# Output-weight parts drawn into step 7, late conditioning pieces moved behind the first output tiles

## Chip, cores and metric

One core of a Trainium2 chip. The metric is the device time of the slowest core in microseconds, here of the only one. The engines are TensorE (PE, its weight loads PEld), VectorE (DVE), ScalarE (ACT), GpSimd (POOL) and SyncE (SP, which issues most DMAs).

## What is computed

One layer of a conditioned decoder trunk in float32, for a prompt of 1024 rows and 8 samples of 8 rows (1088 columns), 1024 channels:

```python
mod = silu(c) @ w_ada + b_ada                      # 6 x 1024 rows: shift, scale, gate for mixer and MLP
h = rms_norm(x, g_mix) * (1 + sc_m) + sh_m
u_val, u_glu, u_rec, u_y = split(h @ w_in + b_in)  # 4 x 512 columns
ya = silu(layer_norm(causal_dwconv31(u_val * sigmoid(u_glu))))
cb = causal_dwconv4(u_rec)
a = exp(-8 * sigmoid(cb @ w_ga) * softplus(-lam))  # gates are block-diagonal
h_t = a * h_(t-1) + sqrt(1 - a^2) * sigmoid(cb @ w_gx) * cb
x = x + gt_m * (concat[ya, h * gelu(u_y)] @ w_out)
h2 = rms_norm(x, g_ffn) * (1 + sc_f) + sh_f
x = x + gt_f * (relu(h2 @ w_up)^2 @ w_down)
y = rms_norm(x, g_final)                           # the last conv rows and h are returned as states too
```

## The kernel before

Every large product is made of three: each float32 operand is split into a high part (ACT, a copy to fp32r, `hi`, line 603) and a low part (POOL, raw minus high, `lo`, line 404), and TensorE adds high x high, high x low and low x high. The order on every engine is written out by hand in five programs (`sync`, `gpsimd`, `scalar`, `vector`, `tensor`) that meet at semaphores.

**In-projection.** Eight steps m = 0..7 of two strips (s = 0, 1) of 128 output columns, each over three chunks c of 384, 384 and 320 token columns. Steps 0 to 3 give value and GLU gate of a quarter j of group A, steps 4 and 5 the recurrent branch, 6 and 7 the GELU branch. Between strips stand pieces of the conditioning product (`ada_piece`, w_ada split too), the means for the LayerNorm (`mean_a`, step 6) and the variances (`var_a`, step 7, line 1530). ACT reads each chunk from PSUM (lines 707 to 710). POOL multiplies value and gate (`product`, line 428), DVE makes the 31 taps of convolution A, one tile j after another (lines 1167 to 1178), then the four taps of convolution B.

**Between step 7 and the output product.** ACT makes the standard deviation (`deviation`, line 811), DVE its reciprocal and the normalised conv_a (`normalise`, lines 1217 and 1218). TensorE makes the gates of the recurrence (`recurrent_gates`), ACT their tanh, a = exp and tanh (`recurrence`, lines 816 to 828), POOL the square a2 (line 498; one buffer, so square j waits for q_done j), DVE the gated input and q (`gated_input`, lines 1224 and 1228), ACT the roots (line 856), DVE the recursion in two halves (`recur`, lines 1262 to 1278), and the low parts of the activations (lines 1283 and 1292). TensorE turns five groups of state rows (`turn_state`, bank 6), read out by DVE (`staged`). Meanwhile the eight blocks k of w_out are loaded into two slots of raw, and split (`w_out_hi`, `w_out_lo`): block k's load waits for the low part of block k - 2.

**Late pieces.** The last 16 of 48 rows of the conditioning are not split: eight `late_piece` q, each eight float32 products of a 128x128 weight block with nine columns (line 1622), that is 16 instructions, into bank 7. DVE adds the bias (line 1312) and makes the second scales sc_f; POOL spreads the MLP gate to the samples.

**Output product and second norm.** `gates` spreads gt_m over the tokens, then nine tiles t of 128 tokens, `tile_product` over eight blocks k (lines 1677 to 1684). Tiles 0 to 3 need half 0 of the activations. Behind tile 1 the last states h_end are turned (line 1710). DVE adds each tile to x (`add_tile`), ACT and DVE make the norm, TensorE turns its rows from behind tile 2 on (`turn`, line 1434), `modulate` applies sc_f. Eight MLP blocks follow.

The program below prints the functions with the lines of the profile.

## Time and profile before

| | |
|---|---|
| median of 3 runs | 1257.45 us (1257.35 to 1257.83) |
| profiled execution | 1255.39 us, span 1253.6 us |
| TensorE busy (matmul) | 1191.2 us, 95% |
| TensorE weight loads | 1070.9 us, 85% |
| DVE busy | 725.8 us, 58% |
| ACT busy | 385.3 us, 31% |
| POOL busy | 346.1 us, 28% |
| mean granted TensorE clock | 0.974 |

The span runs from the first to the last instruction; 1.8 us of the profiled execution lie around it. Busy shares are averages over stages with different limits: what an edit is worth is read from the waits and the timelines of its own stage.
### The profile page before, as it was taken

What the parts mean: (1) busy time and instruction counts of PE and PEld (TensorE: products, weight loads), DVE (VectorE), ACT (ScalarE), POOL (GpSimd) and SP (SyncE); (2) the same over time, 40 slices, a digit from 0 to 9 for tenths busy, and PEclk for the clock granted to TensorE, in tenths of its full rate; (3) what the DMA queues carried; (4) which work ended last, traced back from release to release, by engine and by line L of the source; (5) the groups of instructions that cost most, each with busy time, mean ns of one, the idle gap of its engine ahead of it and who ended that gap; (6) DMA issues with size and microseconds to landing.
All of it is one profiled execution on the core that took longest, in us unless ns stands there. A gap on an engine that the chain in (4) does not pass through costs nothing.

```text
span 1253.6 us, 16249 instructions
## 1 busy us (share of the span) xinstructions
PE 1191.2 (95%) x6255; PEld 1070.9 (85%) x6255; DVE 725.8 (58%) x841; ACT 385.3 (31%) x681; POOL 346.1 (28%) x209
## 2 busy tenths in 40 slices
PE   6789999999869998999999999999999999999996
PEld 2589999988658888989989989989989988988985
DVE  2749999994896555435445445445345345345457
ACT  4842433423762434402302302301301301301322
POOL 0236888440641103302301301301301301301300
PEclk9798999999879998999999999999999999999998
DMA  9524334403415101201201201201201201201112
GB/s 300 176 67 118 101 111 125 118 17 95 127 51 177 35 1 54 69 13 35 85 18 33 84 17 33 84 17 33 84 17 33 84 17 33 84 17 33 50 45 98
DMA packets 80811, 87.36 MB, mean 70 GB/s; under 512 B 3816, under 2 KB 61440, under 8 KB 80771
## 3 DMA queue, kind: packets, MB, share of 16 engines
q1 hardware_dynamic: 78661, 84.77, 21.7%
q10 hardware_dynamic: 2110, 2.05, 0.6%
q8 instruction: 26, 0.43, 0.1%
q14 instruction: 14, 0.11, 0.0%
HBM read 81.72 MB, written 5.08 MB: 69 GB/s over the span
## 4 chain that ended last, share of the span: by engine, by line
PE 86%; DVE 7%; ACT 2%; DMA 2%; issue 2%; POOL 1%; SPq 1%; ACTq 0%; DVEq 0%; POOLq 0%
PE ps L1522 15%; PE ps L1524 15%; PE ps L1523 15%; PE ps L1677 11%; PE ps L1680 11%; PE ps L1678 11%; DMA ada<-in_w_ada 2%; PE ps L1684 1%; PE ps L1683 1%; PE ps L1414 1%; PE ps L1415 1%; PE ps L1530 1%; DVE rstd L1217 1%; DVE tmp_a L1273 1%; DVE gel L1278 0%
## 5 line engine op out<-in xcount | busy, mean ns | idle before, releaser
L1522 PE MATMUL ps<-act_hi,w_hi 128*128 128x384 f32 (+1 forms) x1152 | 380.2, 330 | 10.0 <-POOL w_lo L404 5.6
L1524 PE MATMUL ps<-act_hi,w_lo 128*128 128x384 f32 (+1 forms) x1152 | 377.5, 328 | 0.0
L1523 PE MATMUL ps<-act_lo,w_hi 128*128 128x384 f32 (+1 forms) x1152 | 377.4, 328 | 0.0
L1522 PEld LDWEIGHTS ps<-act_hi,w_hi 128*128 128x128 f32 x1152 | 217.9, 189 | 12.8 <-issue 6.4
L1523 PEld LDWEIGHTS ps<-act_lo,w_hi 128*128 128x128 f32 x1152 | 217.9, 189 | 1.8
L404 POOL TENSOR_TENSOR wb_lo<-raw,wb_hi 128x1024 fp32r<-128x1024 f32 x40 | 98.6, 2474 | 433.3 <-ACT wb_hi L603 433.1
L1524 PEld LDWEIGHTS ps<-act_hi,w_lo 128*128 128x128 f32 x1152 | 217.7, 189 | 0.0
L404 POOL TENSOR_TENSOR w_lo<-raw,w_hi 128x1024 fp32r<-128x1024 f32 x48 | 118.2, 2466 | 334.9 <-ACT w_hi L603 277.8
L1322 DVE TENSOR_TENSOR ps<-ps,gt_p 128x1024 f32<-128x1024 f32 x72 | 88.7, 1232 | 206.8 <-PE ps L1680 206.7
L1677 PE MATMUL ps<-wb_hi 128*128 128x512 f32 x512 | 199.4, 389 | 1.1 <-ACT gt_s L904 1.1
L1678 PE MATMUL ps<-wb_lo,wb_hi 128*128 128x512 f32 x512 | 199.2, 389 | 0.0
L1352 DVE TENSOR_TENSOR relu<-relu 128x384 f32<-128x384 f32 (+1 forms) x96 | 74.7, 778 | 198.7 <-ACT relu L948 198.7
L1680 PE MATMUL ps<-wb_hi,wb_lo 128*128 128x512 f32 x512 | 157.7, 389 | 0.0
L603 ACT ACTIVATE wb_hi<-raw 128x1024 fp32r<-128x1024 f32 x40 | 41.1, 1051 | 360.9 <-PE ps L1684 319.2
L1175 DVE SCALAR_TENSOR_TENSOR ps<-ga,caw,ps 128x1024 f32<-128x1024 f32 x112 | 134.2, 1280 | 0.0
L1677 PEld LDWEIGHTS ps<-wb_hi 128*128 128x128 f32 x512 | 96.1, 188 | 21.1 <-ACT gt_s L904 1.3
L1680 PEld LDWEIGHTS ps<-wb_hi,wb_lo 128*128 128x128 f32 x512 | 96.1, 188 | 20.0
L1678 PEld LDWEIGHTS ps<-wb_lo,wb_hi 128*128 128x128 f32 x512 | 96.1, 188 | 19.7
L948 ACT ACTIVATE relu<-ps 128x384 f32<-128x384 f32 (+1 forms) x96 | 45.2, 471 | 186.6 <-PE ps L1524 177.5
L1324 DVE TENSOR_TENSOR x<-x,ps 128x1024 f32<-128x1024 f32 x72 | 88.0, 1222 | 2.5
L1677 PE MATMUL ps<-wb_hi,act_hi 128*128 128x512 f32 x128 | 51.2, 400 | 11.9 <-DVE act_lo L1292 11.9
L413 POOL TENSOR_TENSOR aw_lo<-raw_ada,aw_hi 128x1024 fp32r<-128x1024 f32 x24 | 57.8, 2427 | 0.0
(229 smaller groups left out, 1287.1 us busy)
## 6 DMA issues: line engine op xcount, KB each, us to landing
raw<-in_w_up SPq DMA_DIRECT2D x32, 512.0 KB, 4.0
raw<-in_w_down SPq DMA_DIRECT2D x32, 512.0 KB, 3.3
raw_ada<-in_w_ada SPq DMA_DIRECT2D x24, 512.0 KB, 3.9
ada<-in_w_ada SPq DMA_DIRECT2D x8, 1024.0 KB, 14.9
x<-in_x_prompt SPq DMA_DIRECT2D x16, 512.0 KB, 8.2
raw<-in_w_in SPq DMA_DIRECT2D x16, 512.0 KB, 5.3
ada_late<-in_w_ada SPq DMA_DIRECT2D x8, 512.0 KB, 4.7
out<-x SPq DMA_DIRECT2D x8, 512.0 KB, 2.6
```

The costliest lines, as they stand in the source:

```text
L404: pool.tensor_tensor(dst, raw[:, slot, :], hi.bitcast(F32), ALU.subtract).then_inc(lo_ready, 1)
L413: pool.tensor_tensor(aw_lo[:, slot, :], raw_ada[:, slot, :], aw_hi[:, slot, :].bitcast(F32), ALU.subtract).then_inc(ada_lo, 1)
L1175: dve.scalar_tensor_tensor(out=out if k == KA - 1 else a, in0=win, scalar=w, in1=a, op0=ALU.mult, op1=ALU.add).then_inc(conva_tap, 1)
L1322: dve.tensor_tensor(src, src, gt_p[:, :], ALU.mult).then_inc(gated, 1)
L1324: dve.tensor_tensor(x2[:, t, :], x2[:, t, :], src, ALU.add).then_inc(rmw_done, 1)
L1352: dve.tensor_tensor(f, r, r, ALU.mult).then_inc(r2_done, 1)
L1522: mm(out, wh, xh, start=(k == 0), stop=False)
L1523: mm(out, wh, xl, start=False, stop=False)
L1524: last = mm(out, wl, xh, start=False, stop=(k == KD - 1))
L1677: mm(out, ah, wh, start=(k == 0), stop=False)
L1678: mm(out, ah, wl, start=False, stop=False)
L1680: last = mm(out, al, wh, start=False, stop=end)
```

## The change

product(0) goes from POOL to DVE, in front of convolution A. In step 7 the variances stand one strip earlier each (behind s = 0 c = 1, s = 0 c = 2 and s = 1 c = 0), and ACT makes the deviations and the first two high parts of w_out behind the first chunk of the last strip. DVE normalises all three chunks in one go. POOL splits w_out blocks 0 and 1 first, waits for all three normalisations (a2 now lies in rstd), and keeps two blocks ahead of the squares; the sample gates follow the squares. ACT takes blocks 2 to 5 between the recurrences, 4 and 5 behind q 1 and q 2. All loads of w_out are on SP. TensorE makes each recurrent gate ahead of the late piece that stood before it. Of the eight late pieces 0 to 2 stay, 3 to 5 stand behind output tile 0, 6 and 7 behind tile 1 ahead of the h_end transposes; the second scales (`late_scales`) stand behind DVE's addition of tile 1, as do the waits for them.

```diff
--- before.py
+++ after.py
@@ -232,7 +232,7 @@
         g_t = [tmp_b[:, j, :] for j in range(J)]
-        a2 = sg
+        a2 = rstd
         gx_t = [tmp_a[:, j, :] for j in range(J)]
@@ -323,16 +323,23 @@
             load_out(0)
+            load_out(1)
             sp.wait_ge(strip_a, 2 * J * NC)
...
             load_late(0, 2)
-            load_out(1)
+            load_out(2)
+            load_out(3)
             sp.wait_ge(strip_b, 2 * J * NC)
...
             load_late(0, 3)
-            for n in range(4):
-                load_out(n + 2)
-                load_late(1, LATE_ORDER[n])
+            load_out(4)
+            load_late(1, 0)
+            load_out(5)
+            load_out(6)
+            load_late(1, 2)
+            load_out(7)
+            load_late(1, 1)
+            load_late(1, 3)
             for a in range(2, LATE):
@@ -457,7 +464,6 @@
-            product(0)
             step(0)
@@ -491,21 +497,25 @@
             pool.wait_ge(var_done, NC)
+            w_out_lo(0)
+            w_out_lo(1)
+            pool.wait_ge(xs_done, NC)
             for j in range(J):
-                w_out_lo(j)
+                if j == 1:
+                    pool.wait_ge(st_tr, 1)
+                w_out_lo(j + 2)
                 pool.wait_ge(a_done, j + 1)
...
                 pool.tensor_tensor(a2[:, :], a_t[j], a_t[j], ALU.mult).then_inc(a2_done, 1)
-                if j == 2:
-                    pool.wait_ge(st_tr, 3)
-                    pool.wait_ge(ada_tr, ADA0 + ADA_S)
-                    pool.wait_ge(ada_evac, ADA0 + ADA_S)
-                    sample_gate(0, M_GTM)
+            pool.wait_ge(st_tr, 3)
+            pool.wait_ge(ada_tr, ADA0 + ADA_S)
+            pool.wait_ge(ada_evac, ADA0 + ADA_S)
+            sample_gate(0, M_GTM)
             pool.wait_ge(evac_a, 2 * J * NC)
...
             pool.wait_ge(q_done, J)
-            for k in range(J, KD):
-                w_out_lo(k)
+            w_out_lo(6)
+            w_out_lo(7)
             for j in range(J):
@@ -734,7 +744,7 @@
                 for c in range(NC):
-                    if c == 2 and 2 <= m <= ADA_S + 1:
+                    if c == (1 if m == 2 * J - 1 else 2) and 2 <= m <= ADA_S + 1:
                         group_out(turned, 7, 0)
@@ -783,6 +793,16 @@
+            def deviation(c):
+
+                t0, w = c * CH, CW[c]
+                act.wait_ge(var_done, c + 1)
+                act.activation(rstd[:, t0:t0 + w], ps[:, 5 + c, 0:w], ACT.Sqrt, bias=eps[:, :]).then_inc(sd_done, 1)
+
+            def w_out_hi(k):
+
+                hi(W_OUT0 + k, k % 2, wb_hi[:, k, :], 16 * ((W_OUT0 + k) // 2 + 1))
+
@@ -793,7 +813,15 @@
-                step(q + J + J // 2, out_a, lambda c, bank: gelu_out(c, bank, 2 * q + 1, evac_b))
+
+                def out_b(c, bank):
+                    gelu_out(c, bank, 2 * q + 1, evac_b)
+                    if last and c == 0:
+                        for n in range(NC):
+                            deviation(n)
+                        w_out_hi(0)
+                        w_out_hi(1)
+                step(q + J + J // 2, out_a, out_b)
@@ -804,12 +832,6 @@
-            def deviation(c):
-
-                t0, w = c * CH, CW[c]
-                act.wait_ge(var_done, c + 1)
-                act.activation(rstd[:, t0:t0 + w], ps[:, 5 + c, 0:w], ACT.Sqrt, bias=eps[:, :]).then_inc(sd_done, 1)
-
@@ -828,24 +850,16 @@
-            def w_out_hi(k):
-
-                hi(W_OUT0 + k, k % 2, wb_hi[:, k, :], 16 * ((W_OUT0 + k) // 2 + 1))
-
-            for c in range(NC):
-                deviation(c)
-            w_out_hi(0)
-            w_out_hi(1)
+            w_out_hi(2)
             recurrence(0)
+            w_out_hi(3)
             recurrence(1)
-            w_out_hi(2)
+            act.wait_ge(q_done, 1)
+            w_out_hi(4)
             recurrence(2)
-            w_out_hi(3)
+            act.wait_ge(q_done, 2)
+            w_out_hi(5)
             recurrence(3)
-            def load_out(k):
-
-                act.wait_ge(lo_ready, W_OUT0 + k - 1)
-                act.dma_start(raw[:, k % 2, :], w_out[0, k * P:(k + 1) * P, :]).then_inc(raw_in[k % 2], 16)
@@ -881,18 +895,12 @@
             roots(0)
-            w_out_hi(4)
-            w_out_hi(5)
+            w_out_hi(6)
+            w_out_hi(7)
             roots(1)
-            load_out(6)
             ya(0)
-            load_out(7)
-            yb_hi(0, 0)
-            yb_hi(0, 1)
-            w_out_hi(6)
-            yb_hi(0, 2)
-            w_out_hi(7)
-            yb_hi(0, 3)
+            for j in range(J):
+                yb_hi(0, j)
             ya(1)
@@ -912,13 +920,14 @@
             act.dma_start(h_sample[0], h_st[1:9, :]).then_inc(staged_out, 16)
-            act.wait_ge(sc_done, 2)
             for t in range(NT):
...
                     strip_hi(W_MLP0 + 1, 1, strip_b, 0)
+                if t == 1:
+                    act.wait_ge(sc_done, 2)
                 if t > 0:
@@ -1179,6 +1188,11 @@
             dve.wait_ge(sa_cp, 2)
+            dve.wait_ge(evac_a, NC)
+            dve.wait_ge(evac_b, NC)
+            dve.tensor_tensor(ga[:, 0, KA - 1:GA_P], ga[:, 0, KA - 1:GA_P], sg[:, 0:SEQ], ALU.mult).then_inc(ga_ready, 1)
+            dve.tensor_tensor(ga_s[:, 0, :, KA - 1:GA_S], ga_s[:, 0, :, KA - 1:GA_S],
+                              sg[:, SEQ:TOK].rearrange("p (b t) -> p b t", t=TB), ALU.mult).then_inc(ga_ready, 1)
             with dve.Fori(0, J) as j:
@@ -1234,12 +1248,11 @@
-            normalise(0)
+            for c in range(NC):
+                normalise(c)
             staged(0, stage[0:KA - 1, 2, :], KA - 1)
-            normalise(1)
             gated_input(0)
             staged(1, stage[0:half_rows, 0, :], half_rows)
-            normalise(2)
             gated_input(1)
@@ -1307,13 +1320,15 @@
-            dve.wait_ge(late_used, 4 * LATE)
-            b_late = par[:, C_BADA + ROW_L:C_BADA + 48].unsqueeze(2).broadcast_to([P, 48 - ROW_L, 9])
-            dve.tensor_tensor(mod[:, ROW_L:48, :], ps[:, 7, 0:9 * (48 - ROW_L)].rearrange("p (r c) -> p r c", c=9),
-                              b_late, ALU.add).then_inc(late_mod, 1)
-            dve.wait_ge(ada_evac, ADA0 + ADA_S)
-            dve.wait_ge(late_mod, 1)
-            scales(sc_f, M_SCF, C_GFFN)
+            def late_scales():
+
+                dve.wait_ge(late_used, 4 * LATE)
+                b_late = par[:, C_BADA + ROW_L:C_BADA + 48].unsqueeze(2).broadcast_to([P, 48 - ROW_L, 9])
+                dve.tensor_tensor(mod[:, ROW_L:48, :], ps[:, 7, 0:9 * (48 - ROW_L)].rearrange("p (r c) -> p r c", c=9),
+                                  b_late, ALU.add).then_inc(late_mod, 1)
+                dve.wait_ge(ada_evac, ADA0 + ADA_S)
+                dve.wait_ge(late_mod, 1)
+                scales(sc_f, M_SCF, C_GFFN)
@@ -1332,12 +1347,14 @@
             dve.wait_ge(gt_cp, 2)
-            dve.wait_ge(sc_done, 2)
             for t in range(NT):
...
                 add_tile(t, out_bank(t), t)
+                if t == 1:
+                    late_scales()
+                    dve.wait_ge(sc_done, 2)
                 if t > 0:
@@ -1559,8 +1576,8 @@
                             mean_a(c)
-                        if last and s == 1:
-                            var_a(c)
+                        if last and 1 <= 3 * s + c <= NC:
+                            var_a(3 * s + c - 1)
@@ -1629,19 +1646,17 @@
             turn_state(0, 6, KA - 1, lambda j: tail_p[:, j, :])
+            recurrent_gates(1)
             late_piece(0)
             turn_state(1, 6, 4 * (KA - 1), lambda j: tail_a[:, j, 0:120])
-            recurrent_gates(1)
+            recurrent_gates(2)
             late_piece(1)
             turn_state(2, 6, 4 * (KA - 1), lambda j: tail_a[:, j, 120:240])
-            recurrent_gates(2)
-            late_piece(2)
+            recurrent_gates(3)
             pe.wait_ge(tails, 2)
             turn_state(3, 6, KB - 1, lambda j: tail_bp[:, j, :])
-            recurrent_gates(3)
+            late_piece(2)
             turn_state(4, 6, NB * (KB - 1), lambda j: tail_b[:, j, :])
-            for q in range(3, 4 * LATE):
-                late_piece(q)
@@ -1704,6 +1719,8 @@
                              (lambda: turn(2, 2, xn[:, 0, :])) if t == 4 else None)
+                for q in ((3, 4, 5), (6, 7))[t] if t < 2 else ():
+                    late_piece(q)
                 if t == 1:
```

## Rows read from the trace of the kernel before

**Rows 1.** TensorE's waits, whole span: line <- releaser: us in total, times, longest

```profile
PE ps L1677 <- DVE act_lo L1292: 11.9, 1, 11.9
...
PE ps L1522 <- POOL w_lo L404: 5.6, 1, 5.6
```

**Rows 2.** timeline of POOL after step 0 (start us, us, engine, operation)

```profile
90.36 2.00 POOL L428 TENSOR_TENSOR ga<-ga,sg 128x1024 f32<-128x1024 f32 x1 [17.07 <-ACT sg L710]
...
92.59 4.70 POOL L404 TENSOR_TENSOR w_lo<-raw,w_hi 128x1024 fp32r<-128x1024 f32 x2
```

**Rows 3.** timeline of ACT after step 0

```profile
89.97 0.31 ACT L710 ACTIVATE sg<-ps,par 128x64 f32<-128x64 f32 x1
90.17 2.00 ACT L778 ACTIVATE w_hi<-raw 128x1024 fp32r<-128x1024 f32 x2
```

**Rows 4.** timeline of DVE: first tap and last addition of convolution A

```profile
92.92 1.35 DVE L1167 TENSOR_SCALAR ps<-ga,caw,par 128x1024 f32 x1 [15.43 <-POOL ga L430]
...
255.92 1.22 DVE L1178 TENSOR_TENSOR conv_a<-conv_a,ps 128x1024 f32 x1
```

**Rows 5.** timeline of TensorE's weight loads: first mean product

```profile
257.31 0.68 PEld L1530 LDWEIGHTS ps<-conv_a,mean_w 128*128 128x128 f32 x3
```

**Rows 6.** chain that ended last, inside step 7 (start us, us, what)

```profile
298.20 2.58 PE ps L1530 x8
```

**Rows 7.** timeline of ACT from the end of step 7 on

```profile
306.33 1.47 ACT L811 ACTIVATE rstd<-ps,eps 128x384 f32<-128x384 f32 x3
...
311.00 0.90 ACT L816 ACTIVATE tmp_a<-ps,hb 128x768 f32<-128x768 f32 x1
...
316.07 0.90 ACT L816 ACTIVATE tmp_a<-ps,hb 128x768 f32<-128x768 f32 x1
```

**Rows 8.** timeline of POOL in the same stretch

```profile
308.91 2.37 POOL L404 TENSOR_TENSOR wb_lo<-raw,wb_hi 128x1024 fp32r<-128x1024 f32 x1 [29.48 <-ACT wb_hi L603]
...
330.43 2.00 POOL L498 TENSOR_TENSOR sg<-tmp_b 128x1088 f32<-128x1088 f32 x1 [3.89 <-DVE tmp_a L1228]
...
344.40 5.97 POOL L404 TENSOR_TENSOR wb_lo<-raw,wb_hi 128x1024 fp32r<-128x1024 f32 x2 [4.13 <-ACT wb_hi L603]
```

**Rows 9.** timeline of DVE in the same stretch

```profile
306.94 2.55 DVE L1217 RECIPROCAL rstd<-rstd 128x384 f32<-128x384 f32 x1 [15.92 <-ACT rstd L811]
309.53 3.37 DVE L1218 TENSOR_TENSOR conv_a<-conv_a,rstd 128x1536 f32<-128x1536 f32 x1
...
320.80 1.28 DVE L1228 SCALAR_TENSOR_TENSOR tmp_a<-sg,tmp_a 128x1088 f32<-128x1088 f32 x1
...
331.47 2.11 DVE L1224 SCALAR_TENSOR_TENSOR tmp_b<-tmp_a,ga 128x1088 f32<-128x1088 f32 x1 [0.58 <-ACT tmp_a L819]
...
341.34 1.28 DVE L1228 SCALAR_TENSOR_TENSOR tmp_a<-sg,tmp_a 128x1088 f32<-128x1088 f32 x1
...
343.49 0.69 DVE L1266 SCALAR_TENSOR_TENSOR tmp_b<-tmp_a,tmp_b 128x512 f32<-128x512 f32 x1
...
364.64 2.48 DVE L1292 TENSOR_TENSOR act_lo<-gel,act_hi 128x512 fp32r<-128x512 f32 x4
```

**Rows 10.** timeline of TensorE: late pieces, then tiles 0 to 2

```profile
336.04 13.98 PE L1622 MATMUL ps<-c_t,ada_late 128*128 128x9 f32 x80
...
367.23 0.77 PE L1677 MATMUL ps<-wb_hi,act_hi 128*128 128x512 f32 x1 [11.91 <-DVE act_lo L1292]
...
390.85 0.48 PE L1677 MATMUL ps<-wb_hi,act_hi 128*128 128x512 f32 x1
...
401.84 1.03 PE L1434 MATMUL ps<-ident,xn 128*128 128x128 f32 x8
```

**Rows 11.** busy us (x instructions) of PE, PEld, DVE, ACT, POOL; clock; DMA

```profile
99.00:100.00 1.00, 1.00 (x5) 1.00 (x4) 1.00 (x2) 0.00 (x0) 1.00 (x2) 0.50 0.93 266
336.00:339.00 3.00, 3.00 (x30) 3.00 (x28) 0.76 (x1) 2.98 (x4) 3.00 (x2) 1.00 0.00 0
341.00:349.00 8.00, 8.00 (x39) 8.00 (x39) 7.75 (x10) 5.96 (x9) 4.53 (x2) 0.50 0.56 155
```

## The prediction

> **What bounds the kernel now.** I read the share of each engine first, then TensorE's waits, then the timelines around the two places where it waits. TensorE is busy 95% of the span, so only what changes its waits or its own work moves the end. It has two waits worth a change: 5.6 us after the first pair of strips and 11.9 us before output tile 0 [rows 1]. Between the first wait's end and the end of step 7 it never idles, and from tile 0 on it is again busy, with every turn of rows to columns following from its own progress. So the end moves by three things: how early or late step 7 is reached, how much sooner tile 0 can start, and what is added to TensorE behind that start. The change touches all three.
>
> **Arrival at step 7.** Removed from POOL: product(0), two instructions, 90.36 to 92.59 [rows 2]. Added to DVE, in front of convolution A. On POOL the first low part of step 1 no longer queues behind them: the high part ends at about 91.2 (half of the two in [rows 3]) and POOL can ask from 91.3 instead of 92.59. TensorE could start step 1 up to 1.1 us earlier. But the convolution on DVE is one unbroken string from 92.92 to 257.14 [rows 4], and the first mean product's weights load at 257.31 [rows 5], 0.17 us after it, exactly where TensorE arrives without waiting. So the convolution decides, and an earlier TensorE would only wait there. When does it start? DVE's long product begins at 90.3 when the sigmoid ends [rows 3] and occupies about 1.2 us (the price of a DVE operation of that length with two SBUF sources, [rows 9], L1228), to 91.5. POOL's low part asks at 91.3 to 91.4. The trace shows that POOL and DVE do not run such operations together: the 1.6 us normalisation that began at 309.53 beside POOL's 308.91 to 311.28 took 3.37 [rows 8, 9], the 1.28 one at 331.47 took 2.11 beside POOL's square to 332.43 [rows 8, 9]; who waits gets the next turn. If POOL gets the turn at 91.5, DVE's short second product (64 columns, about 0.25 us) stands until 93.9 and the convolution starts at 94.4: **+1.5 us**. If DVE slips its short one in first, it starts at about 92.0: DVE would give -0.9, but TensorE, which is at half clock up to about 100.5 ([rows 11]: 0.50 at 99), turns its 1.1 us of head start into about 0.5: **-0.5 us**. The requests are 0.1 to 0.2 us apart, which no row decides: near even, a little for POOL, which asks while DVE still holds.
>
> **Step 7.** The three variance products (2.6, 2.6 and 2.15 us; [rows 6]) change places with strips, so TensorE's work is the same and its last strip ends at 306.3 instead of 304.3. Its last GELU is read out by 307.1 and the gates of the recurrence start there, 0.8 us after the last product (now they follow it at once). In return ACT has the deviations (1.47 us, [rows 7]), two high parts (2.0 us, [rows 3]) and a table load done between strips, where it is idle, and DVE's normalisations start at 299.0 instead of 306.94 [rows 9]. ACT gets one more table load back to GELU inside that idle time; it costs nothing unless the reading of the second strip is late, and then at most its 1.3 us, covered by the strip that runs.
>
> **From there to tile 0** (in the clock of the trace of before, arrival shift left out). ACT: third high part to 308.15, table load, gates from 309.4 instead of 311.00 [rows 7]. One recurrence is 5.07 us (311.00 to 316.07, [rows 7]). DVE: three reciprocals of 2.55 us and three products of 1.6 [rows 9], with POOL's first two low parts (2.37 each, [rows 8]) between them, end at 312.6. POOL now waits for all three normalisations, because its square is written to rstd; queued behind that wait are low part 2 and the first square. Then a cycle repeats, because square j waits for q j: square 2.0, DVE's gated input 1.2 blocked behind it, POOL's next low part 2.35, DVE's q 1.2, together 6.75 us. The first q falls at 321.9 (now 322.0, [rows 9]), the second at 328.6, the third at 335.4; the last has no low part before it and falls at 340.0, against 342.6 now [rows 9]. ACT's two new waits (q 1 and q 2) hold high parts 4 and 5 and the recurrences behind them; these end at 327.9 and 334.7, 0.2 and 0.7 us before the q that follows is due anyway, so they are covered, just. Halves of the roots and two high parts end at 342.5. DVE then has 11.2 us of first-half recursion (2.8 each; it begins with 343.49 now, [rows 9]) and only two low parts beside it instead of four. Two of them back to back took 5.97 and the DVE work beside them was longer by about 3.9 [rows 8], so the recursion ends at 340.7 + 11.2 + 4.3 = 356.2. From its end to tile 0 DVE needs 4.8 us as now (the last 2.48 of it is [rows 9], 364.64). Tile 0 starts at 361.0 instead of 367.23 [rows 10]: **-6.2 us**. Bounds: -11.0 if DVE and POOL never stand in each other's way and only ACT's string counts (q 4 at 335.3), -4 if each low part costs the DVE one more turn. I take -6.2, since both rows with contention show full turns. The modulation gates of TensorE no longer stand behind eight late pieces; they wait for the sample gates at 341.2 and are over by 347, hidden. The six W_out loads go to SP in order; each lands at least 3 us before its high part is due.
>
> **Late pieces.** Five leave a place where TensorE was waiting (80 instructions, 13.98 us from 336.04, [rows 10], before the 11.9 us of idle time) for one where it is not: three behind tile 0, two behind tile 1. At full clock 28 weight loads of 128x128 stand in 3 us [rows 11], 0.107 each, so 16 make 1.71 us and 80 make 8.6; with the changes of kind **+8.7 us**. Nothing takes this up: what follows (x tiles, norms, turns) keeps its distance from tile 1's end, since the h_end transposes that ACT waits for, the addition of tile 1 and turn(0) all stand behind them. The late scales (0.5 us on DVE) now stand behind the addition of tile 1 and end 2.5 us before turn(0) is due: nothing. SP waits for piece 3 with its last late load; queued behind are the state stores (2.4 us) and the x loads. They are due when DVE has the low parts of half 1, about 3 us after piece 3, so x tile 0 may come 0.5 us late, ahead of a DVE that is in no hurry: nothing.
>
> **The clock.** TensorE was busy 8.00 of 8.00 us with late pieces from 341 to 349 and granted 0.50, 1.2 GHz; from 336 to 339 it still had 1.00 [rows 11]. So these pieces, nine columns each, do not hold the clock. Behind tile 0 three of them last 5.2 us. If it falls there, tile 1 starts at half rate. Tile 2 at full rate took 10.99 us (390.85 to 401.84), tiles 0 and 1 together 23.26 with the transposes of 0.36 between them [rows 10]: the cold start of tile 0 cost about 1.2. After step 0 it lasted 5 us, worth 2.6 [rows 11]. A fall costs **0 or about 2 us** (bounds 0 and 3.5, the last if the two pieces behind tile 1 lose it too); near even.
> The Trainium skill (TensorE: Matmul & The Clock Gate, Part 1) says the clock is set by how busy the engine has recently been and that "the default state is throttled, and activity releases the throttle". Read as busy time, that rule would keep the clock through the pieces and give the sum without a fall; the row above speaks against it, with full busy time at half clock.
>
> **Sum.** -6.2 + 8.7 = +2.5; with arrival +1.5 or -0.5 and the clock 0 or +2: +6.0 with both against, +4.0 or +4.0 with one, +2.0 with none. One against is the likeliest. The profiled execution took 1255.39 us (span 1253.6, 1.8 around it), which becomes 1259.3; the median of the runs is 2.06 higher, 1257.45, and becomes 1261.4. A measurement of this kernel can tell about 0.2%, 2.5 us, from no change.
>
> **Rivals.**
> - Forecast: pieces outweigh the earlier start, one of the two coins against: 1261.4, chance 0.40.
> - Both against: 1257.45 + 6.0 = 1263.4, 0.24.
> - Neither: 1259.4, 0.16: within 0.2%.
> - Faster: DVE and POOL get past each other, so that ACT's string alone sets q 4 (335.3), and DVE slips in first after step 0: -11.0 + 8.7 - 0.5 = -2.8, 1254.6. It decides from a start of tile 0 at about 356.5. For it: the requests are fractions of a microsecond apart. Against: every contended row shows a whole turn. 0.10.
> - The rebuild does not do what it says: the q cycle of 6.75 us is no shorter than now, the recursion starts as now and only two low parts are saved beside it: -3.5 + 8.7 + 1.0 = +6, also 1263.5, 0.10; it is told from the others by q 4 at 342 or later.
>
> **How the numbers follow.** Slower: one or both against and the rival without gain, less what their own spread of 1.5 us puts inside 0.2%: 0.66. Same: neither against, and that spread: 0.25. Faster 0.09. The range leaves out the full gain of the faster case and double falls of the clock: 1256.5 to 1265.
>
> **What would show it.** Right: tile 0 starts at 360 to 363; no idle time between it and turn(0), which falls at 404 to 408 instead of 401.84; 80 late matmuls inside; the distance from turn(0) to the end unchanged; the first mean product at 258.8 after a wait on the convolution (or at 256.8 without). Wrong: tile 0 before 357, or late pieces far under 1.7 us each, or a wait that TensorE had between tile 2 and turn(0).

## The result and the profile after

| | before | after |
|---|---|---|
| median of 5 runs | 1257.35 us (1256.04 to 1257.83) | 1265.17 us (1262.26 to 1268.38) |
| ratio | | 1.0061 (95%: 1.0039 to 1.0083) |
| profiled execution | 1255.39 us, span 1253.6 | 1265.32 us, span 1263.5 |

The change makes the kernel 7.8 us slower by the medians and 9.9 us by the two profiled executions. The forecast was +4, its worst case +6. The five runs of the kernel after lie apart, at 1262.26, 1262.30, 1265.17, 1265.32 and 1268.38 us with mean granted clocks of 0.976, 0.976, 0.973, 0.974 and 0.969, so a trace shows one case of what the clock does; the traced one is near the median.

First the share of the engines in the page of the kernel after. TensorE's busy time is the same (1192.0 us of matmul against 1191.2) and the span is ten longer. That doesn't clear the clock: busy time is longer where the clock is low. The five late pieces were busy for 13.98 us before, mostly at half clock, and are busy for 9.05 now, and other products have become longer in their place.

```profile
span 1263.5 us, 16252 instructions
PE 1192.0 (94%) x6255; PEld 1068.1 (85%) x6255; DVE 728.6 (58%) x843; ACT 386.6 (31%) x682; POOL 347.3 (27%) x207
```

TensorE's waits after, whole span (line <- releaser: us in total, times, longest). The first answers to the wait of 11.9 in [rows 1] and has grown, since the late pieces no longer stand in front of it. The last is new: the first mean product now waits for convolution A.

```profile
PE ps L1692 <- DVE act_lo L1305: 13.1, 1, 13.1
...
PE ps L1539 <- POOL w_lo L411: 4.6, 1, 4.6
...
PE ps L1547 <- DVE conv_a L1187: 2.9, 1, 2.9
```

**After step 0.** Timelines of DVE (first three rows, and the last addition of convolution A) and of POOL in the kernel after; they answer to [rows 2 to 4]. POOL's low part begins at 91.67, while DVE's long product still runs; the short product behind it, of 64 columns, takes 2.40 us, and the convolution starts at 94.54 instead of 92.92 and ends at 258.76 instead of 257.14.

```profile
90.71 1.23 DVE L1193 TENSOR_TENSOR ga<-ga,sg 128x1024 f32<-128x1024 f32 x1 [12.92 <-ACT sg L720]
91.85 2.40 DVE L1194 TENSOR_TENSOR ga<-ga,sg 128x64 f32<-128x64 f32 x1
94.54 1.35 DVE L1176 TENSOR_SCALAR ps<-ga,caw,par 128x1024 f32 x1 [0.29 <-DVE ga L1194]
...
257.54 1.22 DVE L1187 TENSOR_TENSOR conv_a<-conv_a,ps 128x1024 f32 x1
```

```profile
91.67 4.84 POOL L411 TENSOR_TENSOR w_lo<-raw,w_hi 128x1024 fp32r<-128x1024 f32 x2 [18.09 <-ACT w_hi L788]
```

**Step 6.** TensorE at the three mean products (which began at 257.49, 265.16 and 272.18 before, none of them waiting), and the windows around the first (the clock is the number behind the five engines). It begins only 1.3 us later than before, but the clock fell while TensorE waited, and the product takes 5.49 us instead of 2.74. The third begins at 276.54 instead of 272.18: 4.36 us late, of which 1.33 are the later start and 3.0 the clock.

```profile
258.82 5.49 PE L1547 MATMUL ps<-conv_a,mean_w 128*128 128x384 f32 x8 [2.94 <-DVE conv_a L1187]
...
269.52 2.74 PE L1547 MATMUL ps<-conv_a,mean_w 128*128 128x384 f32 x8
276.54 2.31 PE L1547 MATMUL ps<-conv_a,mean_w 128*128 128x320 f32 x8
```

```profile
256.00:258.00 2.00, 0.00 (x0) 0.00 (x0) 1.97 (x3) 0.49 (x1) 2.00 (x2) 0.98 0.74 256
258.00:260.00 2.00, 1.18 (x2) 0.84 (x3) 1.71 (x2) 0.00 (x0) 1.62 (x1) 0.50 0.00 0
260.00:262.00 2.00, 2.00 (x4) 1.01 (x3) 2.00 (x5) 0.00 (x0) 0.00 (x0) 0.50 0.00 0
262.00:264.00 2.00, 2.00 (x5) 1.01 (x3) 2.00 (x3) 0.00 (x0) 0.00 (x0) 0.50 0.00 0
264.00:266.00 2.00, 2.00 (x11) 1.90 (x10) 2.00 (x5) 0.00 (x0) 0.00 (x0) 0.81 0.00 0
```

**Between step 7 and tile 0.** Timelines of DVE and POOL after, the counterpart of [rows 8, 9]. The cycle is the forecast one: POOL's square (2.00), DVE's gated input (2.77), POOL's low part (3.44, begun while DVE holds) and DVE's q (3.47, begun while POOL holds) return every 6.7 us.

```profile
322.85 3.47 DVE L1242 SCALAR_TENSOR_TENSOR tmp_a<-rstd,tmp_a 128x1088 f32<-128x1088 f32 x1
...
326.85 2.77 DVE L1238 SCALAR_TENSOR_TENSOR tmp_b<-tmp_a,ga 128x1088 f32<-128x1088 f32 x1
329.54 3.47 DVE L1242 SCALAR_TENSOR_TENSOR tmp_a<-rstd,tmp_a 128x1088 f32<-128x1088 f32 x1
...
342.90 1.32 DVE L1242 SCALAR_TENSOR_TENSOR tmp_a<-rstd,tmp_a 128x1088 f32<-128x1088 f32 x1
```

```profile
326.47 2.00 POOL L509 TENSOR_TENSOR rstd<-tmp_b 128x1088 f32<-128x1088 f32 x1 [1.29 <-DVE tmp_a L1242]
328.42 3.44 POOL L411 TENSOR_TENSOR wb_lo<-raw,wb_hi 128x1024 fp32r<-128x1024 f32 x1
...
346.00 6.01 POOL L411 TENSOR_TENSOR wb_lo<-raw,wb_hi 128x1024 fp32r<-128x1024 f32 x2
```

**Tiles 0 and 1.** TensorE from tile 0 to turn(0), and its windows; they answer to [rows 10]. Tile 0 starts 2.3 us earlier than before, at half clock up to about 370.3, and lasts 13.6 us. The late pieces stand behind the tiles, the clock falls once more at about 384.2, right behind the first three of them (they end at 383.96), and turn(0) comes at 411.26 instead of 401.84, 9.42 us later. From there to the first chunk of 320 columns of the MLP (494.94, before 485.56) the distance is unchanged (83.68 us against 83.72).

```profile
364.92 0.76 PE L1692 MATMUL ps<-wb_hi,act_hi 128*128 128x512 f32 x1 [13.09 <-DVE act_lo L1305]
...
378.54 1.62 PE L1639 MATMUL ps<-c_t,ada_late 128*128 128x9 f32 x14
...
396.42 0.73 PE L1639 MATMUL ps<-c_t,ada_late 128*128 128x9 f32 x6
...
399.91 0.60 PE L1727 MATMUL ps<-ident,h_end 128*9 128x128 f32 x4
...
411.26 0.60 PE L1451 MATMUL ps<-ident,xn 128*128 128x128 f32 x4
```

```profile
364.00:370.00 6.00, 5.08 (x12) 4.05 (x13) 5.61 (x15) 4.75 (x6) 0.90 (x2) 0.50 0.00 0
370.00:372.00 2.00, 2.00 (x9) 1.57 (x9) 1.94 (x3) 0.00 (x0) 0.84 (x2) 0.86 0.00 0
384.00:386.00 2.00, 2.00 (x6) 1.56 (x6) 0.45 (x2) 0.00 (x0) 0.00 (x0) 0.55 1.01 309
386.00:388.00 2.00, 2.00 (x6) 1.54 (x6) 0.00 (x0) 0.00 (x0) 0.00 (x0) 0.59 0.97 299
```

### The profile page after: what moved, and what is told of

It reads as the page before. It is cut to its first block, busy times and chain, and to the rows that moved or that the text cites. A ratio compares the mean times of both kernels' runs of the same rounds, so it can differ in the third digit from the quotient of the medians.

```text
span 1263.5 us, 16252 instructions
## 1 busy us (share of the span) xinstructions
PE 1192.0 (94%) x6255; PEld 1068.1 (85%) x6255; DVE 728.6 (58%) x843; ACT 386.6 (31%) x682; POOL 347.3 (27%) x207
## 4 chain that ended last, share of the span: by engine, by line
PE 74%; issue 11%; DVE 10%; ACT 2%; DMA 2%; DVEq 1%; SPq 1%; ACTq 0%
PE ps L1692 11%; PE ps L1693 11%; PE ps L1695 11%; PE ps L1539 11%; PE ps L1541 11%; PE ps L1540 11%; DVE ps L1184 2%; DMA ada<-in_w_ada 2%; PE ps L1547 1%; PE ps L1699 1%; PE ps L1698 1%; DVE tmp_a L1242 1%; PE ps L1639 1%; DVE tmp_b L1238 1%; PE ps L1451 0%
## 5 line engine op out<-in xcount | busy, mean ns | idle before, releaser
L411 POOL TENSOR_TENSOR wb_lo<-raw,wb_hi 128x1024 fp32r<-128x1024 f32 x40 | 102.3, 2567 | 421.0 <-ACT wb_hi L613 415.0
L1692 PE MATMUL ps<-wb_hi,act_hi 128*128 128x512 f32 x128 | 52.6, 411 | 13.1 <-DVE act_lo L1305 13.1
```

The costliest lines, as they stand in the source:

```text
L411: pool.tensor_tensor(dst, raw[:, slot, :], hi.bitcast(F32), ALU.subtract).then_inc(lo_ready, 1)
L1692: mm(out, ah, wh, start=(k == 0), stop=False)
```

## The experiments

Theory A, which the expectations name, was formed from this trace. The loss has three parts: the turn that POOL takes between DVE's two products, with the clock that the wait at the mean then costs; the late pieces' own time, which no wait hides any more; and the clock in tiles 0 and 1, which starts lower (nothing runs in the wait of 13.1 us) and falls again behind the pieces. Against these stands the gain of the rebuild. The rivals are told with each expectation. Every experiment is the kernel after with the edit shown, but for two that start from the kernel before, and is compared with the kernel before run beside it.

### Where product(0) stands

**e1_product_pool**: the product back on POOL, as before.

```diff
 gpsimd:
+            product(0)
             step(0)
 vector:
-            dve.wait_ge(evac_a, NC)
-            dve.wait_ge(evac_b, NC)
-            dve.tensor_tensor(ga[:, 0, KA - 1:GA_P], ...)
-            dve.tensor_tensor(ga_s[:, 0, :, KA - 1:GA_S], ...)
             with dve.Fori(0, J) as j:
```

> The changed kernel with product(0) back on POOL, all else kept. Theory A (the wait of 2.9 us at the first mean product, made by the later convolution, also costs the clock): the mean starts at about 257.3 without a wait, step 7 ends about 4.4 us sooner, and the time is 4 to 5 us under the changed kernel, near 1260.7. Theory B (only the wait itself counts, 1.5 us; the rest of the delay of step 7 comes from the reordered step 7): 1.5 us under it, near 1263.7.

Measured: 1264.35 us, ratio 1.0059 (1.0043 to 1.0076). The first mean product starts at 257.33 with no wait, the third at 272.03, tile 0 at 360.34 instead of 364.92: the 4.6 us are there. They don't reach the end. The three pieces behind tile 0 start at 374.20 and take 7.98 us instead of 5.42, since the clock now falls inside them and stays at 0.50 up to about 387, and turn(0) comes at 410.15, 1.1 us earlier. In this trace a gain ahead of tile 0 was given back by a longer fall behind it. The total is neither theory's: by its ratio the kernel can't be told from the kernel after (1.0061).

```profile
374.00:376.00 2.00, 2.00 (x19) 1.96 (x18) 2.00 (x2) 0.00 (x0) 2.00 (x2) 1.00 0.00 0
378.00:384.00 6.00, 6.00 (x25) 5.61 (x26) 1.88 (x6) 0.00 (x0) 0.00 (x0) 0.50 1.02 311
384.00:386.00 2.00, 2.00 (x6) 1.53 (x5) 1.23 (x1) 0.00 (x0) 0.00 (x0) 0.50 0.99 358
```

**e2_short_first**: DVE makes the short product ahead of the long one.

```diff
+            dve.tensor_tensor(ga_s[:, 0, :, KA - 1:GA_S], ...)
             dve.tensor_tensor(ga[:, 0, KA - 1:GA_P], ...)
-            dve.tensor_tensor(ga_s[:, 0, :, KA - 1:GA_S], ...)
```

> The changed kernel with DVE's two products in the other order, the short one (64 columns) first. If who waits gets the next turn at the port of DVE and POOL, POOL's low part now waits for the long product only and the convolution starts at about 92.3 instead of 94.54; the mean then waits under 1 us. Theory A: clock kept, 4 to 5 us under the changed kernel. Theory B: about 2. If instead POOL's operation blocks the long product, the convolution starts at 95 or later and the time does not fall.

Measured: 1262.19 us, ratio 1.0043 (1.0026 to 1.006). DVE's timeline in this kernel: the short product takes 0.23 us, no POOL turn comes between the two, and the convolution starts at 92.28.

```profile
90.63 0.23 DVE L1193 TENSOR_TENSOR ga<-ga,sg 128x64 f32<-128x64 f32 x1 [12.93 <-ACT sg L720]
90.77 1.22 DVE L1195 TENSOR_TENSOR ga<-ga,sg 128x1024 f32<-128x1024 f32 x1
92.28 1.35 DVE L1176 TENSOR_SCALAR ps<-ga,caw,par 128x1024 f32 x1 [0.29 <-DVE ga L1195]
```

The mean waits 0.78 us and takes 2.85: a wait that short left the clock at 1.00. The third mean begins at 271.37, 5.2 us before that of the kernel after, and tile 0 at 359.71, but turn(0) at 410.03, only 1.2 earlier: here the clock falls behind tile 0 (0.50 from 378 to 384) and again behind tile 1. Up to tile 0 theory A holds; the total is 2 us under the kernel after by the ratios, theory B's number, and inside the intervals of both.

**e3_fill_wait**: 13 matmuls of 512 columns ahead of the first mean product, into a bank that nobody reads; nothing is left out.

```diff
                         if isinstance(m, int) and m == 2 * J - 2 and s == 1:
+                            if c == 0:
+                                pe.wait_ge(ada_evac, ADA0 + m - 1)
+                                for _ in range(13):
+                                    mm(ps[:, 7, :], w_hi[:, 1, 0:P], act_hi[:, 0, 0:512], start=True, stop=True)
                             mean_a(c)
```

> The changed kernel with 13 extra matmuls of 512 columns (about 2.8 us, result unused) in front of the first mean product, in the time in which TensorE waits for the convolution. Theory A: the mean starts at the same 258.8, but at full clock (2.7 us instead of 5.5), and the time falls by about 2.8 us. Theory B: nothing falls, or it rises by what the extra work overlaps.

Measured: 1263.2 us, ratio 1.0057 (1.004 to 1.0074). TensorE in this kernel at the same place, and the window behind it: the product starts 0.5 us later than in the kernel after, yet the third mean begins at 274.07 against 276.54. From the first mean to the third it is 14.70 us here and 14.69 before, against 17.72 in the kernel after. So the fall of the clock is worth about 3.0 us there, and it hangs on TensorE standing idle, not on when conv_a comes. The total (ratio 1.0057 against 1.0061) doesn't show the gain.

```profile
256.38 3.16 PE L1581 MATMUL ps<-act_hi,w_hi 128*128 128x512 f32 x13
259.37 0.81 PE L1547 MATMUL ps<-conv_a,mean_w 128*128 128x384 f32 x2
```

```profile
258.00:260.00 2.00, 2.00 (x9) 1.50 (x8) 1.71 (x2) 0.00 (x0) 2.00 (x2) 1.00 0.18 74
260.00:262.00 2.00, 2.00 (x8) 1.18 (x7) 2.00 (x3) 0.00 (x0) 0.36 (x1) 1.00 0.00 0
```

**e9_product_dve_only**: the kernel before, with nothing changed but product(0) on DVE.

```diff
 gpsimd:
-            product(0)
             step(0)
 vector:
+            dve.wait_ge(evac_a, NC)
+            dve.wait_ge(evac_b, NC)
+            dve.tensor_tensor(ga[:, 0, KA - 1:GA_P], ...)
+            dve.tensor_tensor(ga_s[:, 0, :, KA - 1:GA_S], ...)
             with dve.Fori(0, J) as j:
```

> The kernel before with only product(0) moved to DVE. Theory A: 4 to 4.5 us slower than before (1.5 later convolution, 2.8 of clock). Theory B: 1.5 us slower.

Measured: 1260.54 us beside 1256.17, ratio 1.0032 (1.0022 to 1.0041), +4.4 us. The mean product waits 2.87 us and takes 5.49 at half clock, the third begins at 276.83, 4.65 us later than before. By the interval this one edit costs 2.8 to 5.2 us, where the later start of the mean alone would cost 1.5 (258.97 against 257.49). The traced execution is the slowest of its ten (1262.15). There turn(0) is 6.0 us later, 407.86, since tile 0 also loses 1.4 us more to its cold start than before, although the late pieces stand where they stood and TensorE waited only 10.22 us ahead of it.

```profile
258.97 5.49 PE L1534 MATMUL ps<-conv_a,mean_w 128*128 128x384 f32 x8 [2.87 <-DVE conv_a L1177]
...
371.85 0.77 PE L1681 MATMUL ps<-wb_hi,act_hi 128*128 128x512 f32 x1 [10.22 <-DVE act_lo L1296]
```

### Where the late pieces stand

**e4_late_back**: the five pieces back behind the last turned state.

```diff
             turn_state(4, 6, NB * (KB - 1), lambda j: tail_b[:, j, :])
+            for q in range(3, 4 * LATE):
+                late_piece(q)
...
-                for q in ((3, 4, 5), (6, 7))[t] if t < 2 else ():
-                    late_piece(q)
```

> The changed kernel with late pieces 3 to 7 back behind the turning of the states, where TensorE waits for the activations anyway. Theory A (80 instructions of 0.107 us on TensorE's path and a fall of the clock behind tile 0): tile 0 starts at the same time, turn(0) about 10.5 us sooner, near 1254.7. Theory B (the pieces cost their own 8.6 us only): near 1256.5. Theory C (the pieces are hidden by waits of DVE and ACT behind tile 0): no change from 1265.2.

Measured: 1251.45 us beside 1257.03, ratio 0.9955 (0.9939 to 0.9972). Tile 0 starts at 364.73, as early as in the kernel after, and with the clock at 1.00; from there to turn(0), 397.96, TensorE needs 33.23 us instead of 46.34. The move of the pieces costs 13.1 us in these traces and 13.4 by the medians, more than theory A's 10.5.

```profile
341.09 11.10 PE L1639 MATMUL ps<-c_t,ada_late 128*128 128x9 f32 x52
...
364.73 0.47 PE L1694 MATMUL ps<-wb_hi,act_hi 128*128 128x512 f32 x1 [0.91 <-issue]
...
386.61 0.60 PE L1727 MATMUL ps<-ident,h_end 128*9 128x128 f32 x4
...
397.96 0.71 PE L1451 MATMUL ps<-ident,xn 128*128 128x128 f32 x5
```

**e5_late_only**: the kernel before with nothing but that move (pieces, second scales and the waits for them).

```diff
             turn_state(4, 6, NB * (KB - 1), lambda j: tail_b[:, j, :])
-            for q in range(3, 4 * LATE):
-                late_piece(q)
...
+                for q in ((3, 4, 5), (6, 7))[t] if t < 2 else ():
+                    late_piece(q)
```

> The kernel before with only the late pieces 3 to 7 and the second scales behind tiles 0 and 1. Tile 0 starts at 367.2 as before, since DVE sets it. A: 10.5 us slower than before. B: 8.6 slower. C: the same as before.

Measured: 1270.35 us, ratio 1.0111 (1.0094 to 1.0128), +13.3 us. Tile 0 starts at 369.21 after a wait of 18.34 us; this execution ran 1.9 us late from step 1 on, so that is the start of before. The wait takes up what the pieces leave; from tile 0 to turn(0) it is 46.87 us instead of 34.61, 12.3 more, where theory A said 10.5; the pieces take 6.25 and 3.63 us behind the tiles.

**e7_rebuild_only**: e1 and e4 together, so the rebuild of step 7 alone.

> The changed kernel with both undone: product(0) on POOL, late pieces where TensorE waits. What is left is the rebuild of step 7 and the recurrence alone. A: tile 0 starts at about 361.0, 6 us sooner than before, and the time is 5 to 7 us under the kernel before, near 1251. If the rebuild gains nothing of its own (its q cycle no shorter): 1257.

Measured: 1249.02 us beside 1257.03, ratio 0.9937 (0.9921 to 0.9954): the rebuild alone brings 8.0 us. The 80 instructions take 17.07 us, all at 0.50, in a place where TensorE waits for DVE anyway, and tile 0 starts behind them at 1.00. It starts at 362.07 in an execution that reached the first mean 1.5 us later than before (259.02 against 257.49, at the same place of the same program); counted from that mean it is 6.7 us earlier than before. e4 differs from this kernel by product(0) alone and is 2.4 us slower by the medians, with intervals that overlap; in its trace the mean waits 2.81 us and takes 4.30, so the wait cost less of the clock there (from the first mean to the third 16.27 us).

```profile
338.00:340.00 2.00, 2.00 (x12) 1.91 (x10) 2.00 (x1) 1.33 (x3) 2.00 (x2) 0.50 1.05 337
340.00:354.00 14.00, 14.00 (x67) 14.00 (x67) 13.56 (x18) 11.97 (x15) 8.97 (x10) 0.50 0.27 84
354.00:362.00 8.00, 6.72 (x40) 6.35 (x39) 7.88 (x12) 5.20 (x7) 0.00 (x0) 0.73 0.00 1
```

**e8_short_late_back**: e2 and e4 together, so the rebuild, the product on DVE in the better order, and the pieces in the wait.

> The changed kernel with DVE's short product first and the late pieces back in the wait ahead of tile 0. Theory A: the convolution starts at 92.3, the first mean product 0.8 us sooner than with product(0) on POOL, so 1248.2, about 0.7% under the kernel before. If the short wait of 0.8 us at the mean product costs the clock after all: 1251.

Measured: 1247.4 us (1246.6 to 1247.6) beside 1257.1, ratio 0.9925 (0.9911 to 0.9938). Its median is the lowest of all, 9.7 us under the kernel before; its interval overlaps that of e7, so the order of the two isn't shown. The convolution starts at 92.32, the mean at 256.89 without a wait, tile 0 at 359.94 and turn(0) at 393.15.

### What the clock does in tiles 0 and 1

**e6_late_spread**: the five pieces one by one between the blocks k of tiles 0 and 1 instead of behind them.

```diff
                             last = mm(out, stk[:, k, :], wl, start=False, stop=end)
+                    if k in between:
+                        late_piece(between[k])
...
-                for q in ((3, 4, 5), (6, 7))[t] if t < 2 else ():
-                    late_piece(q)
+                ... ({3: 3, 5: 4, 6: 5}, {1: 6, 4: 7})[t] if t < 2 else {}
```

> The changed kernel with the five late pieces one by one between the blocks k of tiles 0 and 1, so that no stretch holds only such pieces. A: the clock holds through tile 1 and the time is 1.5 to 2 us under the changed kernel, still some 8.7 us for the pieces. B: no change.

Measured: 1262.68 us, ratio 1.0047 (1.003 to 1.0064). Each piece takes 1.85 us; once the clock is back after tile 0's start it holds 1.00 over all of them, and turn(0) comes at 409.87. Theory A's 1.5 to 2 us are what the ratios give, but within the intervals.

```profile
376.00:386.00 10.00, 10.00 (x62) 8.84 (x61) 9.48 (x16) 1.15 (x4) 2.98 (x2) 1.00 0.70 233
386.00:396.00 10.00, 10.00 (x61) 8.81 (x60) 1.22 (x1) 0.00 (x0) 0.00 (x0) 1.00 1.04 348
```

**e10_warm_tile0**: the kernel after with 46 matmuls of 512 columns behind the gates, so that TensorE isn't idle ahead of tile 0; nobody reads them, nothing is left out.

```diff
             gates(M_GTM, 4, 2)
+            for _ in range(46):
+                mm(ps[:, 6, :], wb_hi[:, 0, 0:P], wb_hi[:, 0, 0:512], start=True, stop=True)
```

> The changed kernel with 46 extra matmuls of 512 columns (10 us, result unused) between the modulation gates and tile 0, in the 13.1 us in which TensorE waits for the activations. Theory A (taking the pieces out of that wait left TensorE cold, and tile 0 pays): tile 0 starts at the same 364.9 but at full clock and takes 10.8 us instead of 13.7, so the time falls by 2.5 to 3 us, to 1262.4. Theory B (the cold start of tile 0 costs no more than it did before the change): it falls by 1.3 us at most.

Measured: 1264.48 us, ratio 1.006 (1.0045 to 1.0076). Tile 0 starts at 364.68 and runs at 1.00, and the pieces begin at 375.65, 2.9 us earlier than in the kernel after. Counted from the start of tile 0 it is 10.97 us instead of 13.62: the cold start, with the clock still at 0.50, costs 2.7 there. The clock has then been 1.00 since 350, for 25 us; TensorE makes the three pieces and it falls, and again at the two behind tile 1. turn(0) comes at 413.19: the gain is given back and more. The traced execution is the slowest of its four (1266.25); by its ratio the kernel can't be told from the kernel after, so theory A's 2.5 to 3 us didn't come.

```profile
364.00:380.00 16.00, 15.32 (x88) 13.47 (x88) 15.15 (x30) 6.08 (x10) 4.70 (x8) 1.00 0.06 17
...
382.00:386.00 4.00, 4.00 (x11) 3.13 (x10) 2.22 (x7) 0.00 (x0) 0.00 (x0) 0.50 0.95 325
...
396.00:398.00 2.00, 2.00 (x18) 2.00 (x18) 0.00 (x0) 0.00 (x0) 0.00 (x0) 0.88 1.19 287
398.00:402.00 4.00, 4.00 (x17) 3.48 (x17) 0.00 (x0) 0.74 (x2) 0.00 (x0) 0.50 0.20 52
```

**e11_pieces_alone**: e1, e6 and e10 together: no wait at the mean, no cold start, no pieces in a row. What is left of the change is the rebuild and the pieces' own time.

> The changed kernel with product(0) on POOL, the late pieces between the blocks of tiles 0 and 1, and the 46 extra matmuls ahead of tile 0: the pieces stay on TensorE's path, but none of the losses of clock do. Theory A: it lies over the kernel with product(0) on POOL and the pieces in the wait (1249.0) by the pieces' own 8.6 us and no more: 1257.6, the time of the kernel before. Theory B (the pieces on the path cost more than their own time in another way): 1260 or more.

Measured: 1257.29 us beside 1257.1, ratio 1.0003 (0.9994 to 1.0013), no difference, as theory A said. The clock is 1.00 from 347 to turn(0) at 402.99. Against e7 (ratio 0.9937) that is 0.66%, 8.3 us, for five pieces on the path.

### The experiments side by side

From the start of tile 0 to turn(0) every kernel does the same work but for the five pieces. Three kernels do it without pieces and at full clock in 33.2 us; e11, with the pieces and at full clock, in 42.4, 9.2 more, five times 1.85. What a kernel needs beyond its 33.2 or 42.4 is the clock.

| kernel | idle ahead of tile 0 | tile 0 | turn(0) | distance | of it clock | at the start of tile 0 | behind pieces |
|---|---|---|---|---|---|---|---|
| before | 11.9 | 367.23 | 401.84 | 34.61 | 1.4 | 1.4 | |
| e9 | 10.2 | 371.85 | 407.86 | 36.01 | 2.8 | 2.8 | |
| e4, e7, e8 | 0.9, 1.4, 1.4 | 364.73, 362.07, 359.94 | 397.96, 395.31, 393.15 | 33.23, 33.24, 33.21 | 0 | 0 | |
| e11 | 2.2 | 360.59 | 402.99 | 42.40 | 0 | 0 | 0 |
| e6 | 13.1 | 364.80 | 409.87 | 45.07 | 2.7 | 2.7 | 0 |
| after | 13.1 | 364.92 | 411.26 | 46.34 | 3.9 | 2.7 | 1.3 |
| e5 | 18.3 | 369.21 | 416.08 | 46.87 | 4.5 | 1.6 | 2.9 |
| e3 | 12.6 | 362.43 | 409.31 | 46.88 | 4.5 | 1.6 | 2.9 |
| e10 | 2.5 | 364.68 | 413.19 | 48.51 | 6.1 | 0 | 6.1 |
| e1 | 12.9 | 360.34 | 410.15 | 49.81 | 7.4 | 2.9 | 4.5 |
| e2 | 12.3 | 359.71 | 410.03 | 50.32 | 7.9 | 1.8 | 6.1 |

The clock's share at the start of tile 0 is the time from there to the first late piece, less the 10.97 us of e10; the rest of its share lies behind pieces. Wherever the pieces stand three and two in a row on the path, the clock falls at them, and with the cold start it costs 3.9 to 7.9 us in these traces. That agrees with e1, e2 and e10: each takes away a real loss ahead of the pieces and gets little of it at the end. Where it isn't nothing, neither share follows a cause that these runs can name. The cold start costs 1.6 us after 18.3 us of idle time (e5) and 2.8 after 10.2 (e9), and the falls cost 1.3 to 6.1 for the same row of pieces. Each line is one execution, and the five runs of the kernel after alone differ by 6.1 us. So that the pieces in a row lose the clock is shown; what a given kernel loses by it, and why, is open. By the medians none of e1, e2, e3, e6 and e10 can be told from the kernel after (ratios 1.0043 to 1.006 against 1.0061 with 1.0039 to 1.0083). What the totals do show is that e5 and e9 are slower than the kernel before, e4, e7 and e8 faster, and e11 as fast.

## Why the prediction was wrong

The sign, and the forecast that the pieces outweigh the earlier start, were right. The size was not: 1265.17 us instead of 1261.4, just past the range's end of 1265.0. Both coins came out against (POOL got the turn, the clock fell), so the forecast's own terms give +6.0, and 3.4 us are missing beyond them, 2.9 of these in the first term. In the clock of the profiled executions:

| term | forecast | after | by |
|---|---|---|---|
| arrival at step 7 | +1.5 or -0.5 | +4.36 | third mean, 276.54 against 272.18 |
| step 7 to tile 0 | -6.2 | -6.67 | tile 0, 364.92 against 367.23, less the 4.36 |
| late pieces | +8.7 | +9.2 | e11 less e4, e7, e8 |
| clock, tiles 0 and 1 | 0 or +2 | +2.5 | 3.9 less before's 1.4 |
| sum | +4, at worst +6 | +9.4 | turn(0), 411.26 against 401.84 |

**Arrival: the step that failed.** The mechanism at the port came as told: POOL gets the turn behind the long product, the convolution starts at 94.54 (told: 94.4), the mean waits and starts at 258.82 (told: 258.8). But the step costed only the lateness of the convolution, +1.5, and put the clock at nothing; the paragraph on the clock looked only at the late pieces. TensorE, ready earlier, stands idle for 2.94 us, the clock halves, and the fp32 mean product and what follows take 3.0 us more: 4.36 instead of 1.5. e3 shows that it is the idle time, e9 that the single edit costs more than 1.5 (+4.4, 2.8 to 5.2), e2 the other side: a wait of 0.78 us costs nothing more. How much of it reaches the end differs: 4.4 us between e9 and before, 2.4 between e4 and e7, and in e1 and e3, with the pieces in a row behind it, none that the medians show.

**Step 7 to tile 0: right.** With the 4.36 of arrival added, the first q ends at 326.3 (told: 321.9 + 4.4), the fourth at 344.2 (340.0 + 4.4), tile 0 starts at 364.92 (361.0 + 4.4 = 365.4). The full turns between DVE and POOL carried this; the rivals in which they get past each other, and in which the cycle is no shorter, fall. e7, the rebuild alone, is 8.0 us faster than before: 6.7 for the earlier start and 1.4 for a tile 0 that starts at full clock.

**Late pieces: right, slightly small.** At full clock a piece takes 1.85 us, not the 1.71 of the weight loads. They are hidden by nothing on the new place (e11), and by TensorE's wait on the old one, where 17.07 us of them at half clock cost nothing (e7). The late scales (ends at 408.45), the last late loads and x cost nothing, as told.

**The clock in tiles 0 and 1: half seen.** The forecast priced one fall behind tile 0. It put the cold start of tile 0 at what it was before (1.2 us by its reading; 23.26 us are tiles 0 and 1 without the transposes, so its own rows give 1.3, and the full-clock kernels 1.4). In the kernel after it costs 2.7, and the fall 1.3, less than the 2 forecast: that the sum of 2.5 lies near the forecast's 2 is luck. The longer cold start isn't explained by the longer idle time ahead of it (13.1 us instead of 11.9), since 10.2 us of it cost 2.8 in e9 and 18.3 cost 1.6 in e5. The fall itself was not a coin: all six traces with three pieces in a row on the path have it, in places and lengths that differ.

The Trainium skill (TensorE: Matmul & The Clock Gate, Part 1) ties the clock to how busy the engine has been. The waits agree: idle for 2.94 us it fell. The pieces don't: in e7 TensorE is busy for 14.00 of 14.00 us from 340 to 354 with 0.50 granted. The same page of the Trainium skill lets activity release the throttle; this stretch is busy all through, and 0.50 stays. Had the rule been used on its other side, for the idle TensorE ahead of the mean, it would have warned of the term that failed.

**The offset.** The forecast added 2.06 us for the median over the profiled execution. The kernel after shows no such offset (1265.32 profiled, 1265.17 median). So +9.4 of the trace, with another 0.5 lost behind turn(0), is +7.8 in the medians, and the terms missed by 5.4 us where the final number missed by 3.8. That the offset was absent made the miss smaller by luck.

## What to carry to other kernels

A new wait of TensorE can cost its delay and the clock behind it, so price both. Small-column float32 products belong where TensorE waits anyway, even at half clock, or singly between full-rate products, and not in a row on its path. Where two engines share a port and one hands over between two operations, put the short operation first. When an edit ahead of such a row of products brings less than its trace promises, look at the clock behind it before doubting the edit, and compare several executions, since one trace shows one case of the clock.

## What the hardware showed that was not expected

- A wait of 2.94 us (2.87 in e9, 2.81 in e4) drops the granted clock to 0.50 (1.2 GHz) within the wait, and it is back only some 6 us after work resumes (3 in e4): 5.49 us for a product of 2.74 (4.30 in e4). After 0.78 us it stays at 1.00.
- Products of nine columns hold TensorE busy without a gap and still lose the clock, or don't get it back: 80 in a row take 17.07 us at 0.50, as five groups of 16 between full-rate blocks 5 x 1.85 us at 1.00. With 25 us of full clock ahead of them (e10) they lose it all the same.
- The same cold start can cost 1.4 or 2.8 us: behind the start of tile 0 the clock came back at about 370.2 before (start 367.23) and 377.8 in e9 (start 371.85), the second after the shorter idle time.
- An operation of 64 columns on DVE took 2.40 us behind POOL's turn and 0.23 us in front of it. The Trainium skill (SBUF — State Buffer, SBUF: two separate sides) calls the shared port pair "an exclusive lock, not a bandwidth split"; the traces agree (after, e9, e4, and e2 for the order), and add who comes next: the engine that asked while the other held, here POOL from 91.67.
